# Experts of 65 to 128 tokens: the down projection as plain fp32 products, with only w1 and w3 split into high and low parts

## The chip, the cores and the metric

The kernel runs on one core of one Trainium2 chip. The metric is the device time in microseconds (us); the kernel before takes 2081.54 us, the median of three runs from 2077.73 to 2081.86 us. A change of about 0.2% of that, some 4 us, is what a measurement of this kernel can tell from no change.

## The reference, cut to what matters

Two layers of a token mixer and a channel mixer run over 256 context and 256 latent tokens of width 1024. The channel mixer of the second layer is a mixture of eight experts with the two best chosen for each token, and it is this part that the change touches:

```python
def swiglu(h, w1, w3, w2):
    return (jax.nn.silu(h @ w1) * (h @ w3)) @ w2

def moe_swiglu(h, w_r, w1e, w3e, w2e):
    logits = (h @ w_r).astype(jnp.float32)
    vals, idx = lax.top_k(logits, TOP_K)          # TOP_K = 2
    ...
    for e in range(N_EXPERTS):                    # 8
        out = out + comb[..., e:e + 1] * swiglu(h, w1e[e], w3e[e], w2e[e])
```

The inputs and weights are float32. Of one expert w1 and w3 are 1024 x 3584 and w2 is 3584 x 1024, so each expert brings 44 MB of weights.

## The kernel before, in words

The first part of the program, to about 1090 us, is everything up to the routing. After it come the eight experts, one after the other. For each expert the number of tokens that chose it (at most 256) is read into a register on every engine, and `by_width` branches to one of three programs: `few` for up to 64 tokens, `mid` for 65 to 128, and `big` for more. The code of all three is written out for each of the eight experts; an engine jumps over the ones it does not need. The code of one expert stands in the order few, mid, big.

The hidden width of 3584 is cut into seven blocks (`NB`) of 512 (`BLK`). A block has six pieces of weights of 128 x 2048 float32 words, 1 MiB each: pieces 0 to 3 are w1 and w3 for the two halves of the 1024 input rows, pieces 4 and 5 are the 512 rows of w2. SyncE (SP) loads them one by one into a ring of ten slots (`ESLOTS`), in the order of `ORDER` (lines 72 and 73), in which the two w2 pieces of block b-1 stand behind the four gate and up pieces of block b. A slot is loaded again when the matmuls that read it have ended (`wait_free`, line 532 and 536 are the two DMA issues). So the next expert's first ten pieces can land while the present one ends.

`mid` reaches float32 accuracy from TensorE's rounded format fp32r. A number is written as a high part, which is its value rounded to fp32r, and a low part, which is the rest; a product is then three products: high by high, low by high and high by low. For each of the 42 pieces of an expert

- ScalarE (ACT) copies the landed piece into one of three buffers `highs`, as rounded words (line 1370, `split`), once the piece used three before has been used up;
- VectorE (DVE) subtracts that from the piece in its place in the ring (line 1462, called by `split`), which leaves the low part there;
- TensorE (PE) runs `piece_product` (line 983 on): four times high by high (line 992) and low by high (line 994) from `highs`, and then four times high by low (line 999) from the ring. That is twelve matmuls of 128 x 128 weights by 128 x 512 moving words.

The order on PE within block b is: pieces 0 and 1 (`hidden(b, 0)`), four transposes of the gated hidden values of block b-1 (`turn`, line 1020), pieces 2 and 3 (`hidden(b, 1)`), and the two w2 pieces of block b-1 (`down`), which sum into the two banks `ps[0]` and `ps[1]` over all blocks. ACT applies the Silu (line 1376), DVE multiplies (line 1922) into `hid`; after the transposes ACT takes the high part `eh_high` from the bank (line 1380), and DVE the low part `eh_low` (line 1462 again, as a 128x512 form). At the end of an expert the order is: the first half of the next expert's gather (line 877), `turn` of the last block, `down` of the last two blocks, the second half of the gather, a transpose of the routing weights (line 884), and sixteen matmul records that spread the result over the tokens (line 902, `add_slots`), which need the copies of the two banks by ACT (line 1391) and DVE (line 1941).

`few` uses the pieces as they land, as fp32 products without any splitting: its gate and up matmuls are line 922, its down matmuls line 948. Its tiles have 64 columns of weights, and two of them stand beside each other in the array. In the runs' data three experts take `mid` (the first, the second and the fifth), five take `few`, none takes `big`.

Of the kernel before, what the change touches and what calls it, by code (L numbers as in the profile page):

```python
# [17 lines left out]
F32 = mybir.dt.float32  # L18
# [9 lines left out]
P = 128  # L28
D = 1024
# [36 lines left out]
BLK = 512  # L66
# [8 lines left out]
ORDER += [(NB - 1, 4), (NB - 1, 5)]  # L75
PLACE = {piece: n for n, piece in enumerate(ORDER)}
PER = len(ORDER)
HIGHS = 3

STEPS = 2 * NB  # L80
# [113 lines left out]
def hybrid_backbone(nc, x, c, ctx_in, c_ctx, w_mod, b_mod, g_mix_pre, g_mix_post, w_in, w_decay, b_decay, gla_norm,  # L194
# [23 lines left out]
    with ExitStack() as stack:  # L218
# [93 lines left out]
        spare_words = mixT[:, :, :].rearrange("p a b -> p (a b)")  # L312
        hid = spare_words[:, 0:2 * BLK].rearrange("p (a n) -> p a n", a=2)
        eh = spare_words[:, 2 * BLK:4 * BLK].rearrange("p (a n) -> p a n", a=2)
        rounded_words = x_high[:, :, :].rearrange("p a b -> p (a b)")
        eh_high = rounded_words[:, 2 * BLK:4 * BLK].rearrange("p (a n) -> p a n", a=2)
        eh_low = rounded_words[:, 4 * BLK:6 * BLK].rearrange("p (a n) -> p a n", a=2)
        highs = [x_low[:, 0:4, :].rearrange("p a b -> p (a b)"), x_low[:, 4:8, :].rearrange("p a b -> p (a b)"),
                 norms_r[:, 2:6, :].rearrange("p a b -> p (a b)")]

# [58 lines left out]
        high_ready = sem("high_ready")  # L379
        high_used = sem("high_used")  # L380
        low_ready = sem("low_ready")
        eh_low_ready = sem("eh_low_ready")
        sel_ready = sem("sel_ready")
        gather_ready = sem("gather_ready")
        xsel_vector = sem("xsel_vector")
# [174 lines left out]
        def _(pe):  # L560
# [345 lines left out]
            def few(e):  # L906

                H = FEW
                x = xsel
                pe.sem_inc(extra_ready, 3)  # L910
                pe.sem_inc(high_used, PER)

                def hidden(b, half):
                    acc = ps[2 + b % 2]
                    if half == 0 and b >= 2:
                        pe.wait_ge(hid_ready, e * STEPS + 2 * (b - 2) + 2)
                    for w in range(2):
                        wait_piece(pe, e, b, 2 * half + w)
                    for kk in range(4):
                        k = 4 * half + kk  # L920
                        for w in range(2):
                            ins = pe.matmul(acc[H * w:H * w + H, :], x[:, k, 0:H],  # L922
                                            piece_words(e, b, 2 * half + w)[:, kk * BLK:(kk + 1) * BLK],
                                            start=(k == 0), stop=(k == KD - 1), skip_group_check=True)
                            if kk == 3:
                                frees(ins, e, b, 2 * half + w)
                    if half == 1:
                        ins.then_inc(gu_ready, 2)

                def turn(b):  # L930

                    pe.wait_ge(hid_ready, e * STEPS + 2 * b + 2)
                    if b >= 2:
                        pe.wait_ge(eh_ready, e * STEPS + 2 * (b - 2) + 2)
                    for q in range(2):
                        ins = pe.transpose(ps[6 + b % 2][:, q * P:(q + 1) * P],  # L936
                                           hid[:, b % 2, q * P:(q + 1) * P], ident[:])
                    ins.then_inc(turn_ready, 2)

                def down(b):  # L940
                    pe.wait_ge(eh_ready, e * STEPS + 2 * b + 2)
                    for i in range(2):
                        wait_piece(pe, e, b, 4 + i)
                        for jj in range(2):
                            j = 2 * i + jj
                            for half in range(2):
                                o = jj * D + half * BLK
                                ins = pe.matmul(ps[0][H * half:H * half + H, :],  # L948
                                                eh[:, b % 2, ((j % 2) * 2 + j // 2) * H:][:, 0:H],
                                                piece_words(e, b, 4 + i)[:, o:o + BLK],  # L950
                                                start=(b == 0 and j == 0), stop=(b == NB - 1 and j == 3),
                                                skip_group_check=True)
                        frees(ins, e, b, 4 + i)
                    return ins

                pe.wait_ge(xsel_vector, e + 1)
                pe.wait_ge(xsel_scalar, e + 1)
                if e:
                    pe.wait_ge(sum_done, 4 * e)
                for b in range(NB):  # L960
                    hidden(b, 0)
                    if b:
                        turn(b - 1)
                    hidden(b, 1)
                    if b < NB - 1 and b:
                        down(b - 1)
                next_gather(e, 0)
                turn(NB - 1)
                down(NB - 2)
                down(NB - 1).then_inc(y_ready, STEPS)  # L970
                next_gather(e, 1)
                if e + 1 < NE:
                    turn_weights(e + 1)

                pe.wait_ge(y_vector, STEPS * (e + 1))
                pe.wait_ge(y_scalar, STEPS * (e + 1))
                add_slots(e, lambda s, m: yslot[H * (m // 4):H * (m // 4) + H, 0, (m % 4) * P:(m % 4 + 1) * P],
                          lambda s, m: swt_up[H:2 * H, :] if m // 4 else swt[0:H, e % 2, :], 1)

            def mid(e):  # L980
# [2 lines left out]

                def piece_product(b, i, outs, high, low, first, last):

                    n = e * PER + PLACE[b, i]
                    w_high_ = highs[n % HIGHS]
                    w_low_ = piece_words(e, b, i, ring_r)
                    pe.wait_ge(high_ready, n + 1)
# [25 lines left out]
                def turn(b):  # L1015
                    pe.wait_ge(hid_ready, e * STEPS + 2 * b + 2)
                    if b >= 2:
                        pe.wait_ge(eh_low_ready, e * STEPS + 2 * (b - 2) + 2)
                    for j in range(4):
                        ins = pe.transpose(ps[6 + b % 2][:, j * P:(j + 1) * P], hid[:, b % 2, j * P:(j + 1) * P],  # L1020
                                           ident[:])
# [1 line left out]

                def down(b):
                    pe.wait_ge(eh_ready, e * STEPS + 2 * b + 2)
                    pe.wait_ge(eh_low_ready, e * STEPS + 2 * b + 2)
                    for i in range(2):
                        js = [2 * i + q // 2 for q in range(4)]
                        ins = piece_product(b, 4 + i, [ps[q % 2][:] for q in range(4)],
                                            [eh_high[:, b % 2, j * P:(j + 1) * P] for j in js],  # L1030
                                            [eh_low[:, b % 2, j * P:(j + 1) * P] for j in js],
                                            2 if b == 0 and i == 0 else 0, 2 if b == NB - 1 and i == 1 else 0)
                    return ins

                pe.wait_ge(xsel_vector, e + 1)
# [21 lines left out]

            def big(e):

                pe.sem_inc(high_used, PER)  # L1060
                pe.wait_ge(xsel_vector, e + 1)
                pe.wait_ge(xsel_scalar, e + 1)
                if e:
# [84 lines left out]
        def _(act):  # L1148
# [193 lines left out]

            def few(e):
                H = FEW
                act.sem_inc(high_ready, PER)
                for b in range(NB):
                    act.wait_ge(gu_ready, e * STEPS + 2 * b + 2)
                    if b >= 2:
# [10 lines left out]
            def mid(e):  # L1359

                def split(n):

                    if n < PER:
                        b, i = ORDER[n]
                        at_ = e * PER + n
                        wait_piece(act, e, b, i)
                        if at_ >= HIGHS:
                            act.wait_ge(high_used, at_ - HIGHS + 1)
# [8 lines left out]

                def turned(b):
                    act.wait_ge(turn_ready, e * STEPS + 2 * b + 2)
                    act.copy(eh_high[:, b % 2, :], ps[6 + b % 2][:]).then_inc(eh_ready, 2)  # L1380

                for n in range(PER + 2):
                    split(n)
                    used = ORDER[n - 2] if n >= 2 else None
                    if used is not None and used[1] == 3:
                        gate(used[0])
                    if used is not None and used[1] == 1 and used[0]:
# [6 lines left out]

            def big(e):

                act.sem_inc(high_ready, PER)
                for b in range(NB):
                    for s in range(2):
                        act.wait_ge(gu_ready, e * STEPS + 2 * b + s + 1)  # L1400
# [22 lines left out]
        def _(dve):  # L1423
# [456 lines left out]
            def few(e):  # L1880
                H = FEW
                dve.sem_inc(extra_done, 3)
                dve.sem_inc(low_ready, PER)
                dve.sem_inc(eh_low_ready, STEPS)
                dve.wait_ge(swt_done, e + 1)
                dve.tensor_copy(swt_up[H:2 * H, :], swt[0:H, e % 2, :])
                for b in range(NB):
# [18 lines left out]
            def mid(e):  # L1906
                dve.sem_inc(extra_done, 3)

                def split(n):

                    if n < PER:
                        b, i = ORDER[n]
                        at_ = e * PER + n
                        dve.wait_ge(high_ready, at_ + 1)
                        low_part(piece_words(e, b, i, ring_r), piece_words(e, b, i),
                                 highs[at_ % HIGHS].bitcast(F32)).then_inc(low_ready, 1)
# [5 lines left out]
                    dve.tensor_tensor(hid[:, b % 2, :], esg[:, b % 2, :], ps[3 + 2 * (b % 2)][:],  # L1922
                                      ALU.mult).then_inc(hid_ready, 2)

                def turned(b):
                    dve.wait_ge(eh_ready, e * STEPS + 2 * b + 2)
                    low_part(eh_low[:, b % 2, :], ps[6 + b % 2][:],
                             eh_high[:, b % 2, :].bitcast(F32)).then_inc(eh_low_ready, 2)

                for n in range(PER + 2):  # L1930
                    split(n)
                    used = ORDER[n - 2] if n >= 2 else None
                    if used is not None and used[1] == 3:
                        gate(used[0])
                    if used == (2, 0) and e + 1 < NE:
                        select(e + 1)
                    if used is not None and used[1] == 1 and used[0]:
                        turned(used[0] - 1)
                turned(NB - 1)
                dve.wait_ge(y_ready, STEPS * (e + 1))  # L1940
                dve.tensor_copy(yslot[:, 0, 512:1024], ps[1][:]).then_inc(y_vector, STEPS)
                if e + 1 < NE:
# [3 lines left out]

            def big(e):

                dve.sem_inc(low_ready, PER)
                dve.sem_inc(eh_low_ready, STEPS)  # L1950
                for half in range(2):
                    dve.wait_ge(extra_ready, 3 * e + half + 1)
                    dve.tensor_copy(xsel2[:, 4 * half:4 * half + 4, :],
# [62 lines left out]
```

## Time and profile before

| what | value |
|---|---|
| median of three runs | 2081.54 us |
| the profiled execution: its own time | 2080.61 us |
| its span, first to last instruction | 2078.8 us |
| TensorE busy | 1827.6 us (88%) |
| VectorE busy | 844.4 us (41%) |
| ScalarE busy | 487.2 us (23%) |
| mean granted TensorE clock | 0.93 of 2.4 GHz |
| read from memory | 473.38 MB, 228 GB/s over the span |

A record of a matmul lasts from its start to its modelled end, which includes the way through the array, so successive matmuls overlap in the records; the distance between two starts is what a matmul costs in a row of them. An fp32 matmul has two records in the trace (and two weight loads), an fp32r matmul has one. "issue" as the releaser of an idle time says that the profile shows nothing that the engine waited for.

### The profile page before, as it was taken

What the parts mean: (1) busy time and instruction counts of PE and PEld (TensorE: products, weight loads), DVE (VectorE), ACT (ScalarE), POOL (GpSimd) and SP (SyncE); (2) the same over time, 40 slices, a digit from 0 to 9 for tenths busy, and PEclk for the clock granted to TensorE, in tenths of its full rate; (3) what the DMA queues carried; (4) which work ended last, traced back from release to release, by engine and by line L of the source; (5) the groups of instructions that cost most, each with busy time, mean ns of one, the idle gap of its engine ahead of it and who ended that gap; (6) DMA issues with size and microseconds to landing.
All of it is one profiled execution on the core that took longest, in us unless ns stands there. A gap on an engine that the chain in (4) does not pass through costs nothing.

```text
span 2078.8 us, 19529 instructions
## 1 busy us (share of the span) xinstructions
PE 1827.6 (88%) x7982; PEld 1131.9 (54%) x7982; DVE 844.4 (41%) x1212; ACT 487.2 (23%) x568; POOL 2.3 (0%) x12
## 2 busy tenths in 40 slices
PE   5998888969999999799779979997876998787886
PEld 2344444438888777348667868842324884232322
DVE  1243242073434466424448868820203882020102
ACT  3211023110000000221327747600002760000001
POOL 0000000000000000000000000000000000000000
PEclk9899999979999999899779999999998999999988
DMA  9323089142232220331237969979999997999994
GB/s 345 106 81 122 0 320 368 61 142 81 93 110 71 81 74 0 122 121 41 82 122 285 375 222 375 363 281 395 394 394 363 376 354 289 395 393 393 394 395 183
DMA packets 223827, 476.20 MB, mean 229 GB/s; under 512 B 9906, under 2 KB 32724, under 8 KB 223700
## 3 DMA queue, kind: packets, MB, share of 16 engines
q1 hardware_dynamic: 222176, 474.24, 62.3%
q8 instruction: 85, 1.39, 0.3%
q10 hardware_dynamic: 1524, 0.21, 0.1%
q14 instruction: 42, 0.34, 0.0%
HBM read 473.38 MB, written 1.05 MB: 228 GB/s over the span
## 4 chain that ended last, share of the span: by engine, by line
PE 70%; SPq 12%; DMA 7%; DVE 6%; issue 4%; ACT 2%; ACTq 0%; DVEq 0%; POOL 0%; POOLq 0%
PE ps L633 11%; SPq L532 9%; PE ps L639 6%; PE ps L640 6%; PE ps L641 6%; PE ps L992 6%; PE ps L994 6%; PE ps L922 5%; PE ps L999 5%; PE ps L794 4%; DMA ring<-in_e_w 4%; PE ps L685 3%; SPq L536 3%; DMA ring<-in_w_mod 3%; PE ps L588 3%
## 5 line engine op out<-in xcount | busy, mean ns | idle before, releaser
L922 PE MATMUL ps<-ring,work 128*64 128x512 f32 x1120 | 283.1, 655 | 83.1 <-DMA ring<-in_e_w 66.1
L633 PE MATMUL ps<-hT,ring 128*128 128x512 f32 (+2 forms) x672 | 246.9, 527 | 22.0 <-issue 12.3
L922 PEld LDWEIGHTS ps<-ring,work 128*64 128x64 f32 x1120 | 92.1, 149 | 250.0 <-issue 250.0
L633 PEld LDWEIGHTS ps<-hT,ring 128*128 128x128 f32 (+1 forms) x672 | 129.0, 196 | 137.5 <-issue 117.6
L1462 DVE TENSOR_TENSOR ring_rounded<-ring,hT_rounded 128x2048 fp32r<-128x2048 f32 x84 | 191.6, 2289 | 29.2 <-ACT hT_rounded L1370 22.0
L1894 DVE TENSOR_TENSOR mixT<-work,ps 64x256 f32<-64x256 f32 x70 | 29.7, 424 | 425.1 <-ACT work L1351 424.0
L1370 ACT CAST hT_rounded<-ring 128x2048 fp32r<-128x2048 f32 x84 | 159.9, 1911 | 45.0 <-PE ps L994 34.2
L639 PE MATMUL ps<-mixT_rounded,work_rounded 128*128 128x512 f32 x352 | 140.6, 399 | 10.6 <-DVE hT_rounded L1462 10.6
L641 PE MATMUL ps<-mixT_rounded,ring_rounded 128*128 128x512 f32 x352 | 139.1, 395 | 0.0
L640 PE MATMUL ps<-hT_rounded,work_rounded 128*128 128x512 f32 x352 | 139.1, 395 | 0.0
L948 PE MATMUL ps<-ring,mixT 128*64 128x512 f32 x560 | 125.8, 593 | 0.0
L992 PE MATMUL ps<-hT_rounded,work_rounded 128*128 128x512 f32 x252 | 102.2, 406 | 21.8 <-issue 18.6
L1462 DVE TENSOR_TENSOR ring_rounded<-ring,norms_rounded 128x2048 fp32r<-128x2048 f32 x42 | 96.1, 2289 | 22.7 <-ACT norms_rounded L1370 22.7
L994 PE MATMUL ps<-hT_rounded,work_rounded 128*128 128x512 f32 x252 | 100.2, 398 | 1.8 <-issue 1.8
L999 PE MATMUL ps<-ring_rounded,work_rounded 128*128 128x512 f32 x336 | 90.5, 391 | 0.2 <-DVE ring_rounded L1462 0.2
L794 PE MATMUL ps<-mixT,ring 128*128 128x512 f32 (+1 forms) x256 | 85.0, 486 | 1.2 <-issue 1.2
L1462 DVE TENSOR_TENSOR ring_rounded<-ring,work_rounded 128x1024 fp32r<-128x1024 f32 (+1 forms) x88 | 84.1, 956 | 1.5
L639 PEld LDWEIGHTS ps<-mixT_rounded,work_rounded 128*128 128x128 f32 x352 | 67.2, 191 | 30.0 <-DVE hT_rounded L1462 10.8
L948 PEld LDWEIGHTS ps<-ring,mixT 128*64 128x64 f32 x560 | 41.6, 137 | 76.1 <-issue 70.2
L1370 ACT CAST norms_rounded<-ring 128x2048 fp32r<-128x2048 f32 x42 | 80.3, 1913 | 9.3 <-issue 6.9
L588 PE MATMUL ps<-norms,ones 128*128 128x512 f32 (+1 forms) x144 | 69.0, 611 | 13.3 <-ACT norms L1178 13.2
L1353 ACT COPY mixT<-ps 128x256 f32<-128x256 f32 x35 | 13.0, 372 | 269.7 <-PE ps L936 269.7
(221 smaller groups left out, 2311.7 us busy)
## 6 DMA issues: line engine op xcount, KB each, us to landing
ring<-in_e_w SPq DMA_DIRECT2D x336, 1024.0 KB, 13.8
ring<-in_w_mod SPq DMA_DIRECT2D x24, 2048.0 KB, 15.9
ring<-in_w_in SPq DMA_DIRECT2D x12, 2048.0 KB, 11.8
ring<-in_w SPq DMA_DIRECT2D x22, 1024.0 KB, 7.8
ring<-in_w_out SPq DMA_DIRECT2D x4, 2048.0 KB, 13.9
ring<-in_w SPq DMA_DIRECT2D x4, 2048.0 KB, 7.8
ring<-in_w SPq DMA_DIRECT2D x2, 1536.0 KB, 6.5
mixT<-in_ctx SPq DMA_DIRECT2D x2, 512.0 KB, 4.2
```

Of the source, the lines that this page charges most:

```text
L532: sp.dma_start(dst.rearrange("p (k n) -> p k n", k=4), rows(w[0, e, k0 * P:(k0 + 4) * P], b * BLK, BLK)).then_inc(piece_in[s], 16)
L633: ins = pe.matmul(acc[0:width, 0:TOK - c0], w[:, k, m * P:m * P + width], hT[:, k, c0:], start=(k == 0), stop=(k == KD - 1))
L639: pe.matmul(acc, w_high_, x_high_, start=first, stop=False)
L640: pe.matmul(acc, w_high_, x_low_, start=False, stop=False)
L641: return pe.matmul(acc, w_low_, x_high_, start=False, stop=last)
L794: ins = pe.matmul(acc[:, 0:n], w[:, k, (m % 4) * P:(m % 4 + 1) * P], mixT[:, k, c0:], start=(i == 0), stop=(i == KD - 1))
L922: ins = pe.matmul(acc[H * w:H * w + H, :], x[:, k, 0:H], piece_words(e, b, 2 * half + w)[:, kk * BLK:(kk + 1) * BLK], start=(k == 0), stop ...
L992: pe.matmul(outs[q], high[q], w_high_[:, cols], start=q < first, stop=False, skip_group_check=True)
L994: ins = pe.matmul(outs[q], low[q], w_high_[:, cols], start=False, stop=False, skip_group_check=True)
L999: ins = pe.matmul(outs[q], high[q], w_low_[:, q * BLK:(q + 1) * BLK], start=False, stop=q >= 4 - last, skip_group_check=True)
L1370: act.copy(highs[at_ % HIGHS], piece_words(e, b, i)).then_inc(high_ready, 1)
L1462: return dve.tensor_tensor(dst, src, high, ALU.subtract)
```

## The change

Only the program `mid` changes in what it computes with. The gate and up pieces (w1 and w3) are split as before. The w2 pieces are no longer split: PE multiplies them as they lie in the ring, as fp32, by the transposed hidden values, which ACT now copies as plain float32 words into `eh`. The low part of the hidden values, its semaphore and DVE's step for it are gone. The counters of the splitting run over the 28 gate and up pieces (`SPLIT`) and not over all 42 (`PER`). The order of the pieces in the ring, their loading, and the order of the steps on PE stay.

```diff
+SPLIT = len(GATE_UP)
...
 (TensorE, mid)
                 def turn(b):
                     pe.wait_ge(hid_ready, e * STEPS + 2 * b + 2)
                     if b >= 2:
-                        pe.wait_ge(eh_low_ready, e * STEPS + 2 * (b - 2) + 2)
+                        pe.wait_ge(eh_ready, e * STEPS + 2 * (b - 2) + 2)
...
                 def down(b):
                     pe.wait_ge(eh_ready, e * STEPS + 2 * b + 2)
-                    pe.wait_ge(eh_low_ready, e * STEPS + 2 * b + 2)
                     for i in range(2):
-                        js = [2 * i + q // 2 for q in range(4)]
-                        ins = piece_product(b, 4 + i, [ps[q % 2][:] for q in range(4)],
-                                            [eh_high[:, b % 2, j * P:(j + 1) * P] for j in js],
-                                            [eh_low[:, b % 2, j * P:(j + 1) * P] for j in js],
-                                            2 if b == 0 and i == 0 else 0, 2 if b == NB - 1 and i == 1 else 0)
+                        wait_piece(pe, e, b, 4 + i)
+                        for jj in range(2):
+                            j = 2 * i + jj
+                            for half in range(2):
+                                o = jj * D + half * BLK
+                                ins = pe.matmul(ps[half][:], eh[:, b % 2, j * P:(j + 1) * P],
+                                                piece_words(e, b, 4 + i)[:, o:o + BLK],
+                                                start=(b == 0 and j == 0), stop=(b == NB - 1 and j == 3),
+                                                skip_group_check=True)
+                        frees(ins, e, b, 4 + i)
                     return ins
...
 (ScalarE, mid)
                 def split(n):
-                    if n < PER:
-                        b, i = ORDER[n]
-                        at_ = e * PER + n
+                    if n < SPLIT:
+                        b, i = GATE_UP[n]
+                        at_ = e * SPLIT + n
...
                 def turned(b):
                     act.wait_ge(turn_ready, e * STEPS + 2 * b + 2)
-                    act.copy(eh_high[:, b % 2, :], ps[6 + b % 2][:]).then_inc(eh_ready, 2)
-
-                for n in range(PER + 2):
+                    act.copy(eh[:, b % 2, :], ps[6 + b % 2][:]).then_inc(eh_ready, 2)
+
+                for n in range(SPLIT + 2):
                     split(n)
-                    used = ORDER[n - 2] if n >= 2 else None
+                    used = GATE_UP[n - 2] if n >= 2 else None
...
 (VectorE, mid)
-                def turned(b):
-                    dve.wait_ge(eh_ready, e * STEPS + 2 * b + 2)
-                    low_part(eh_low[:, b % 2, :], ps[6 + b % 2][:],
-                             eh_high[:, b % 2, :].bitcast(F32)).then_inc(eh_low_ready, 2)
-
-                for n in range(PER + 2):
+                for n in range(SPLIT + 2):
```

## Rows read from the trace of the kernel before

**Rows 1.** The page: span, engines' busy time, DMA issues of the experts' weights.
```profile
span 2078.8 us, 19529 instructions
PE 1827.6 (88%) x7982; PEld 1131.9 (54%) x7982; DVE 844.4 (41%) x1212; ACT 487.2 (23%) x568; POOL 2.3 (0%) x12
...
ring<-in_e_w SPq DMA_DIRECT2D x336, 1024.0 KB, 13.8
```

**Rows 2.** Busy time by engine in stretches; the last three columns are clock, DMA share, GB/s.
```profile
core 0: us, PE busy (x) PEld busy (x) DVE busy (x) ACT busy (x) POOL busy (x), PEclk, DMA share, GB/s
1160.00:1200.00 40.00, 40.00 (x183) 33.07 (x182) 35.88 (x20) 28.31 (x18) 0.00 (x0) 1.00 1.02 376
...
1400.00:1440.00 40.00, 30.30 (x132) 11.03 (x132) 1.70 (x4) 2.29 (x5) 0.00 (x0) 0.96 1.04 395
...
1098.80:1221.10 122.30, 120.28 (x548) 99.17 (x549) 104.07 (x60) 84.87 (x56) 0.00 (x0) 1.00 0.95 346
...
1369.80:1587.30 217.50, 180.36 (x800) 70.48 (x800) 26.71 (x57) 17.74 (x35) 0.00 (x0) 0.93 1.01 381
```

**Rows 3.** Waits of TensorE over the first `mid` expert: total, times, longest.
```profile
PE ps L992 <- issue: 1.4, 1, 1.4
PE ps L1020 <- DVE mixT L1922: 0.4, 1, 0.4
PE ps L999 <- DVE ring_rounded L1462: 0.2, 1, 0.2
```

**Rows 4.** Timeline, TensorE in a steady `mid` block: start, duration, line.
```profile
1132.93 0.48 PE L992 MATMUL ps<-hT_rounded,work_rounded 128*128 128x512 f32 x1
...
1137.59 1.07 PE L999 MATMUL ps<-ring_rounded,work_rounded 128*128 128x512 f32 x4
...
1140.31 1.07 PE L999 MATMUL ps<-ring_rounded,mixT_rounded 128*128 128x512 f32 x4
...
1149.73 0.48 PE L992 MATMUL ps<-hT_rounded,work_rounded 128*128 128x512 f32 x1
```

**Rows 5.** Timeline, fp32 matmuls of layer 0's output projection, full clock.
```profile
373.24 7.03 PE L794 MATMUL ps<-mixT,ring 128*128 128x512 f32 x16
380.11 1.02 PE L588 MATMUL ps<-norms,ones 128*128 128x512 f32 x2
```

**Rows 6.** Timeline, down matmuls of a `few` expert.
```profile
1409.08 3.63 PE L948 MATMUL ps<-ring,mixT 128*64 128x512 f32 x16
```

**Rows 7.** Timeline, TensorE at the end of the first `mid` expert.
```profile
1205.71 1.95 PE L877 MATMUL ps<-work 128*128 128x128 f32 x16
1208.06 0.65 PE L1020 MATMUL ps<-ident,mixT 128*128 128x128 f32 x4 [0.41 <-DVE mixT L1922]
...
1213.12 1.07 PE L999 MATMUL ps<-ring_rounded,mixT_rounded 128*128 128x512 f32 x4
1215.58 0.47 PE L992 MATMUL ps<-hT_rounded,mixT_rounded 128*128 128x512 f32 x1 [1.39 <-issue]
```

**Rows 8.** The same end, on ScalarE and VectorE.
```profile
1212.46 0.57 ACT L1380 CAST mixT_rounded<-ps 128x512 fp32r<-128x512 f32 x1
1212.59 2.29 DVE L1462 TENSOR_TENSOR ring_rounded<-ring,norms_rounded 128x2048 fp32r<-128x2048 f32 x1 [1.92 <-ACT norms_rounded L1370]
1214.80 0.68 DVE L1462 TENSOR_TENSOR mixT_rounded<-ps,mixT_rounded 128x512 fp32r<-128x512 f32 x1
```

**Rows 9.** TensorE's first matmuls of the experts 1, 2, 4 and 5, with the idle time ahead.
```profile
1234.66 0.76 PE L992 MATMUL ps<-hT_rounded,work_rounded 128*128 128x512 f32 x1 [7.56 <-issue]
1369.78 12.22 PE L922 MATMUL ps<-ring,work 128*64 128x512 f32 x48 [3.62 <-issue]
1598.26 0.77 PE L992 MATMUL ps<-hT_rounded,work_rounded 128*128 128x512 f32 x1 [11.00 <-issue]
1731.70 12.22 PE L922 MATMUL ps<-ring,work 128*64 128x512 f32 x48 [3.79 <-issue]
```

**Rows 10.** Waits of the DMA queue SP over the expert part.
```profile
SPq L532 <- PE ps L999: 280.8, 84, 43.6
SPq L536 <- PE ps L999: 104.6, 42, 4.0
```

**Rows 11.** ScalarE's split of a piece and ScalarE's Silu in the steady state.
```profile
1133.75 1.92 ACT L1370 CAST norms_rounded<-ring 128x2048 fp32r<-128x2048 f32 x1
1138.74 0.60 ACT L1376 ACTIVATE work<-ps 128x512 f32<-128x512 f32 x1 [1.26 <-issue]
```

More of the change, by code:

```diff
@@ L314, in hybrid_backbone @@
         eh = spare_words[:, 2 * BLK:4 * BLK].rearrange("p (a n) -> p a n", a=2)
-        rounded_words = x_high[:, :, :].rearrange("p a b -> p (a b)")
-        eh_high = rounded_words[:, 2 * BLK:4 * BLK].rearrange("p (a n) -> p a n", a=2)
-        eh_low = rounded_words[:, 4 * BLK:6 * BLK].rearrange("p (a n) -> p a n", a=2)
         highs = [x_low[:, 0:4, :].rearrange("p a b -> p (a b)"), x_low[:, 4:8, :].rearrange("p a b -> p (a b)"),
@@ L381, in hybrid_backbone @@
         low_ready = sem("low_ready")
-        eh_low_ready = sem("eh_low_ready")
         sel_ready = sem("sel_ready")
@@ L910, in few @@
                 pe.sem_inc(extra_ready, 3)
-                pe.sem_inc(high_used, PER)
+                pe.sem_inc(high_used, SPLIT)
                 def hidden(b, half):
@@ L984, in piece_product @@
                 def piece_product(b, i, outs, high, low, first, last):
-                    n = e * PER + PLACE[b, i]
+                    n = e * SPLIT + GATE_UP.index((b, i))
                     w_high_ = highs[n % HIGHS]
@@ L1058, in big @@
             def big(e):
-                pe.sem_inc(high_used, PER)
+                pe.sem_inc(high_used, SPLIT)
                 pe.wait_ge(xsel_vector, e + 1)
@@ L1344, in few @@
                 H = FEW
-                act.sem_inc(high_ready, PER)
+                act.sem_inc(high_ready, SPLIT)
                 for b in range(NB):
@@ L1395, in big @@
             def big(e):
-                act.sem_inc(high_ready, PER)
+                act.sem_inc(high_ready, SPLIT)
                 for b in range(NB):
@@ L1882, in few @@
                 dve.sem_inc(extra_done, 3)
-                dve.sem_inc(low_ready, PER)
-                dve.sem_inc(eh_low_ready, STEPS)
+                dve.sem_inc(low_ready, SPLIT)
                 dve.wait_ge(swt_done, e + 1)
@@ L1909, in split @@
                 def split(n):
-                    if n < PER:
-                        b, i = ORDER[n]
-                        at_ = e * PER + n
+                    if n < SPLIT:
+                        b, i = GATE_UP[n]
+                        at_ = e * SPLIT + n
                         dve.wait_ge(high_ready, at_ + 1)
@@ L1923, in gate @@
                                       ALU.mult).then_inc(hid_ready, 2)
-                def turned(b):
-                    dve.wait_ge(eh_ready, e * STEPS + 2 * b + 2)
-                    low_part(eh_low[:, b % 2, :], ps[6 + b % 2][:],
-                             eh_high[:, b % 2, :].bitcast(F32)).then_inc(eh_low_ready, 2)
-                for n in range(PER + 2):
+                for n in range(SPLIT + 2):
                     split(n)
-                    used = ORDER[n - 2] if n >= 2 else None
+                    used = GATE_UP[n - 2] if n >= 2 else None
                     if used is not None and used[1] == 3:
@@ L1936, in mid @@
                         select(e + 1)
-                    if used is not None and used[1] == 1 and used[0]:
-                        turned(used[0] - 1)
-                turned(NB - 1)
                 dve.wait_ge(y_ready, STEPS * (e + 1))
@@ L1947, in big @@
             def big(e):
-                dve.sem_inc(low_ready, PER)
-                dve.sem_inc(eh_low_ready, STEPS)
+                dve.sem_inc(low_ready, SPLIT)
                 for half in range(2):
```

## The prediction, made before the changed kernel had run

> **What bounds the kernel now.** I read the page first, to see which engine is busiest: TensorE (PE) at 88%, and eight experts that load 336 MiB-sized pieces, 42 each [rows 1]. That average mixes two kinds of expert, so next come the stretches [rows 2]. In a `few` expert the DMA moves 395 GB/s at a share of 1.04 and PE is busy 30 of 40 us: the load of weights sets the pace. In a `mid` expert PE is busy 40.0 of 40.0 us at a clock of 1.00 (the 2.4 GHz level), while the DMA moves 376 GB/s and 346 over the whole first expert. So here PE sets the pace, but not by much: a block of six pieces is 6.29 MB, which at 395 GB/s is 15.9 us, and PE takes 1149.73 - 1132.93 = 16.80 us for it [rows 4]. PE's waits settle it: over the first `mid` expert nowhere does PE wait for a DMA, and its waits on VectorE (DVE) and for nothing visible sum to 2.0 us [rows 3]; the other way round SP waits 385 us for matmuls of line 999 to free slots [rows 10]. DVE is at 35.9 of 40 us and ScalarE (ACT) at 28.3 [rows 2]; both wait for PE's use of the buffers, so their work counts only where PE waits for them.
>
> **What the change takes from PE.** Per block `down` runs two pieces of twelve fp32r matmuls. A piece takes 1140.31 - 1137.59 = 2.72 us [rows 4], 0.227 us a matmul. Two pieces are 5.44 us.
>
> **What it adds to PE.** Per block 8 fp32 matmuls of 128x128 by 128x512, 16 records. The same shape stands in layer 0 at full clock: 16 records fill 380.11 - 373.24 = 6.87 us [rows 5], 0.859 us a matmul. These have their own weight load in each record too, so it is inside the figure. Operands of the same kind (one tile of weights for two halves, other banks) give no reason for another rate, and I take 6.87 us. Net per block: 6.87 - 5.44 = +1.43 us. There are seven blocks in each of three `mid` experts: 21 x 1.43 = +30.0 us.
>
> The bounds: below, two fp32 matmuls with 64 columns of weights run beside each other in `few`, 16 records in 3.63 us [rows 6]; that needs half-width tiles, which `down` of `mid` has not. Above, a full-width fp32 matmul could cost four times an fp32r one as these run here, 4 x 0.227 = 0.907 us, so 7.25 us a block, +1.81, and 21 x 1.81 = +38.1. The row of the same shape is the nearest, so 0.859 stands. The trace shows 0.859 / 0.227 = 3.79 fp32r matmuls for one fp32 matmul, against the three that the split form uses. The Trainium skill (FP8 and Floating Point Precision, TensorE Precision Notes) says that true fp32 makes four passes through the array where the reduced form makes one, which speaks against this change; the trace nearly agrees, and by the rule at fp32r's distance the net would be that upper 38.1.
>
> **What it takes from ACT and DVE.** Two copies of 1.92 us from ACT [rows 11], two subtractions of 2.29 us and one of 0.68 from DVE [rows 8] per block, 5.3 us of DVE. In the steady block PE waits for neither, so 18 of these 21 blocks gain nothing. At an expert's end they do matter. DVE is in the subtraction of a w2 piece when the last gate is due; `turn` of the last block waits 0.41 us for it [rows 7]. Then, between `down` of block 5 and `down` of block 6, PE stands still: the last line 999 group starts at 1213.12 and would pass on after 4 x 0.227 = 0.91 us, at 1214.03, but the next matmul starts at 1215.58 [rows 7], 1.55 us late. What it waits for is the low part of the hidden values, which DVE takes only at 1214.80, behind the split of the first w2 piece, ending at 1215.48 [rows 8]. Both waits go: ACT's float copy follows the transposes at once and is done some 6 us before `down` of block 6, which stands behind 6.87 us of matmuls. The three `mid` experts look alike here, so 3 x (1.55 + 0.41) = -5.9 us. What is late next is nothing on ACT or DVE: with three buffers of high parts and 28 pieces, they get three pieces ahead during each `down`; a gate-up piece then asks 2.29 of DVE per 2.72 us of PE and of ACT 1.92, and the gates' 0.68 and 0.60 us [rows 8, 11] fit in the 6.87 us of `down`.
>
> **The DMA and the slots.** Issue order and count stay. A w2 piece is now freed after its own 3.43 us of matmuls in place of 2.72, so PE asks for a block each 18.23 us where the DMA needs 15.9: nothing new waits there, and SP's waits on PE grow. Nor does a `few` expert give it back: it begins with a full ring before and after, and runs at 395 GB/s already. So the sum stays on the path.
>
> **Sum.** +30.0 - 5.9 = +24.1 us. On the profiled execution: span 2078.8 to 2102.9, its own time 2080.6 to 2104.7. The median of the runs is 0.9 above that execution, so 2105.6 us.
>
> **Rivals.**
> (a) The gate-up matmuls get faster, since DVE and ACT touch memory less. An fp32r matmul takes 0.227 us and one record pass of fp32 half of 0.429, so 0.215: if all 48 fp32r matmuls left in a block fell to that, 48 x 0.012 x 21 = -12.1 us, +12 in all, 2093.5. For it: the split form alone has the longer distance. Against: nothing says that the other engines cause it, since PE's starts are as regular where DVE pauses.
> (b) The four stalls behind a branch. PE stands 7.56, 3.62, 11.0 and 3.79 us before its first matmul of the next expert, mostly for nothing that the profile shows [rows 9]; the code of `mid` gets shorter, and where it lies moves. The spread between like branches (3.6 to 11.0) is 7.4 us; two such moves the wrong way give +24 + 15 = +39, 2120, the right way +9, 2091. The Trainium skill (Runtime: NRT & Kernel Launch, Instruction fetch mechanics) says that a taken branch out of the fetched window makes the engine wait for its code; the stalls fit that, and no row tells how the shorter code would change them.
> (c) The other side, faster: fp32 matmuls on neighbouring banks overlap as in [rows 6], 3.63 us for a block's `down`. PE would need 16.80 - 5.44 + 3.63 = 15.0 us a block, the DMA's 15.9 decides, and 21 x (16.80 - 15.9) = 19 us go: 2063. It decides if 16 records take under 5.4 us. Against it: [rows 5] shows full-width ones, one behind the other.
> (d) No change: the DMA is the real bound and covers a slower PE. It would need DMA waits on PE in `mid`; [rows 3] has none. 2081.5.
>
> **How the numbers follow.** Forecast 0.82 (2098 to 2114, the upper end by the 0.907 us bound with the end's gain: +32), (a) 0.06, (b) 0.07, of which half is above the range, (c) 0.03, (d) 0.02. Range 2094 to 2115. Slower by over 0.2% holds the forecast, (a) and (b): 0.95; same 0.02; faster 0.03. The 0.2%, 4 us, is what a measurement of this kernel can tell.
>
> **What would show it.** Right: line 992, 994 and 999 with 336 records each in place of 504, 336 new records of an fp32 matmul from the ring at a distance of 0.43 us, a steady block of 18.2 us, the DMA rate in a `mid` stretch down to about 6.29 MB / 18.2 us = 345 GB/s, the stop before the last `down` gone, DVE near 25 of 40 us, the `few` stretches as long as before. Wrong: a block of 16 us or less (c), a distance below 0.22 us between gate-up matmuls (a), other stalls ahead of the first matmul of an expert (b), PE waiting for DMA or for DVE in the steady block.

## The result, and the profile after

The changed kernel takes 2100.81 us, the median of five runs (2099.38 to 2105.08), against 2081.54 for the kernel before beside it: a ratio of 1.0095, 95% interval 1.0077 to 1.0112, so 16 to 23 us slower. Five more runs on another occasion gave 1.012 (1.0102 to 1.0137), 21 to 29 us. The +24.1 us that was forecast lies 1 us above the first interval and inside the second. The profiled execution's span went from 2078.8 to 2103.2 us, +24.4; that execution, at 2105.08 us, was the slowest of its five.

The page of the changed kernel, its first lines and the group of the new down matmuls (line, engine, operation, tiles, count, busy time, mean ns):

```profile
span 2103.2 us, 19020 instructions
PE 1865.7 (89%) x7814; PEld 1099.7 (52%) x7814; DVE 738.0 (35%) x1149; ACT 409.2 (19%) x526; POOL 2.3 (0%) x12
...
L1030 PE MATMUL ps<-ring,mixT 128*128 128x512 f32 x336 | 147.1, 592 | 0.0
```

VectorE lost 106 us of work and ScalarE 78, against [rows 1], and PE gained 38 us of recorded busy time: work left two engines that had waited and came to the one that had not.

A steady block of the changed kernel on PE (timeline; the records of a few matmuls in between are left out):

```profile
1135.67 0.60 PE L1018 MATMUL ps<-ident,mixT 128*128 128x128 f32 x4
...
1141.60 7.03 PE L1030 MATMUL ps<-ring,mixT 128*128 128x512 f32 x16
...
1150.29 1.07 PE L997 MATMUL ps<-ring_rounded,work_rounded 128*128 128x512 f32 x4
...
1153.01 1.07 PE L997 MATMUL ps<-ring_rounded,work_rounded 128*128 128x512 f32 x4
1153.92 0.60 PE L1018 MATMUL ps<-ident,mixT 128*128 128x128 f32 x4
```

From `turn` to `turn` a block is 1153.92 - 1135.67 = 18.25 us, against 16.80 in [rows 4]. Sixteen fp32 records last 7.03 us from the first start to the last modelled end, to the hundredth what line 794 showed in [rows 5]. A gate-up piece still takes 2.72 us.

The stretch of the changed kernel that answers to [rows 2], same columns:

```profile
1160.00:1200.00 40.00, 40.00 (x145) 26.41 (x145) 22.50 (x13) 19.38 (x14) 0.00 (x0) 1.00 0.98 351
```

PE is full and at the 2.4 GHz level, as before. DVE fell from 35.9 to 22.5 of 40 us, the DMA from 376 to 351 GB/s, since PE asks for less.

The end of the first expert, and the first matmul of the next, which answer to [rows 7] and [rows 9]:

```profile
1214.57 1.95 PE L875 MATMUL ps<-work 128*128 128x128 f32 x16
...
1216.35 0.60 PE L1018 MATMUL ps<-ident,mixT 128*128 128x128 f32 x4
1216.79 13.90 PE L1030 MATMUL ps<-ring,mixT 128*128 128x512 f32 x32
1230.52 1.95 PE L875 MATMUL ps<-work 128*128 128x128 f32 x16
...
1244.40 0.76 PE L990 MATMUL ps<-hT_rounded,work_rounded 128*128 128x512 f32 x1 [7.91 <-issue]
```

Both `down` run as one group of 32 records; neither the wait ahead of `turn` nor the stop ahead of the last `down` is left.

Where the 24.4 us of the two profiled spans lie, each `mid` expert from its first matmul to the second half of the gather:

| stretch | before | after | more |
|---|---|---|---|
| expert 0 (mid) | 1098.85 to 1221.14 | 1100.54 to 1230.52 | 7.7 |
| expert 1 (mid) | 1234.66 to 1360.19 | 1244.40 to 1376.07 | 6.1 |
| expert 4 (mid) | 1598.26 to 1721.95 | 1614.23 to 1745.32 | 7.4 |
| all the rest | | | 3.2 |

The three `mid` experts hold 21.2 us. The rest is 1.7 ahead of the experts, 0.4 between experts 0 and 1, 0.1 from expert 1's gather to expert 4 and 1.0 behind expert 4, outside the products that were changed. The same three stretches in the second profile of the changed kernel are 130.01, 131.84 and 130.94 us, 21.3 in sum over the kernel before, while its stretch ahead of the experts is 1.0 us shorter than before: that part varies from execution to execution.

### The profile page after: what moved, and what is told of

It is laid out like the page before. It is cut to its first block, busy times and chain, and to the rows that moved or that the text cites. A ratio compares the mean times of both kernels' runs of the same rounds, so it can differ in the third digit from the quotient of the medians.

```text
span 2103.2 us, 19020 instructions
## 1 busy us (share of the span) xinstructions
PE 1865.7 (89%) x7814; PEld 1099.7 (52%) x7814; DVE 738.0 (35%) x1149; ACT 409.2 (19%) x526; POOL 2.3 (0%) x12
## 4 chain that ended last, share of the span: by engine, by line
PE 72%; SPq 11%; DMA 6%; DVE 6%; issue 3%; ACT 1%; ACTq 0%; DVEq 0%; POOL 0%; POOLq 0%
PE ps L631 11%; SPq L530 8%; PE ps L1030 7%; PE ps L920 6%; PE ps L637 6%; PE ps L639 6%; PE ps L638 6%; DMA ring<-in_e_w 4%; PE ps L792 4%; PE ps L990 4%; PE ps L992 4%; PE ps L997 4%; PE ps L683 3%; SPq L534 3%; PE ps L586 3%
## 5 line engine op out<-in xcount | busy, mean ns | idle before, releaser
L920 PE MATMUL ps<-ring,work 128*64 128x512 f32 x1120 | 292.2, 672 | 74.9 <-DMA ring<-in_e_w 58.1
L631 PE MATMUL ps<-hT,ring 128*128 128x512 f32 (+2 forms) x672 | 246.5, 526 | 22.5 <-issue 12.3
L1464 DVE TENSOR_TENSOR ring_rounded<-ring,hT_rounded 128x2048 fp32r<-128x2048 f32 x57 | 129.8, 2290 | 108.3 <-ACT hT_rounded L1372 107.4
L1030 PE MATMUL ps<-ring,mixT 128*128 128x512 f32 x336 | 147.1, 592 | 0.0
L638 PE MATMUL ps<-hT_rounded,work_rounded 128*128 128x512 f32 x352 | 139.1, 395 | 0.0
L1372 ACT CAST hT_rounded<-ring 128x2048 fp32r<-128x2048 f32 x57 | 107.9, 1906 | 95.9 <-issue 70.4
L990 PE MATMUL ps<-hT_rounded,work_rounded 128*128 128x512 f32 x228 | 96.7, 424 | 21.3 <-issue 18.1
L1030 PEld LDWEIGHTS ps<-ring,mixT 128*128 128x128 f32 x336 | 63.5, 190 | 73.0 <-issue 71.8
L992 PE MATMUL ps<-hT_rounded,work_rounded 128*128 128x512 f32 x228 | 90.7, 398 | 0.0
L637 PEld LDWEIGHTS ps<-mixT_rounded,work_rounded 128*128 128x128 f32 x352 | 67.2, 191 | 29.8 <-DVE hT_rounded L1464 10.8
L639 PEld LDWEIGHTS ps<-mixT_rounded,ring_rounded 128*128 128x128 f32 x352 | 67.3, 191 | 14.3
```

The source lines that it names most:

```text
L631: ins = pe.matmul(acc[0:width, 0:TOK - c0], w[:, k, m * P:m * P + width], hT[:, k, c0:], start=(k == 0), stop=(k == KD - 1))
L637: pe.matmul(acc, w_high_, x_high_, start=first, stop=False)
L638: pe.matmul(acc, w_high_, x_low_, start=False, stop=False)
L639: return pe.matmul(acc, w_low_, x_high_, start=False, stop=last)
L920: ins = pe.matmul(acc[H * w:H * w + H, :], x[:, k, 0:H], piece_words(e, b, 2 * half + w)[:, kk * BLK:(kk + 1) * BLK], start=(k == 0), stop ...
L990: pe.matmul(outs[q], high[q], w_high_[:, cols], start=q < first, stop=False, skip_group_check=True)
```

## Experiments

The theory: PE alone sets the pace in a `mid` expert; the fp32 form costs it 1.43 us a block, and the work taken from ScalarE and VectorE counts only at two stops at an expert's end. The rivals: the splitting slows PE in other ways; the price is per expert and not per block; the DMA decides.

**Only the end of an expert, with everything still split.** In the loops of ScalarE and VectorE over the pieces:

```diff
                 for n in range(PER + 2):
+                    if n == PER - 3:          # VectorE alone
+                        gate(NB - 1)
+                    if n == PER - 1:          # both
+                        turned(NB - 1)
                     split(n)
...
-                    if used is not None and used[1] == 3:
+                    if used is not None and used[1] == 3 and used[0] < NB - 1:      # VectorE alone
...
-                turned(NB - 1)
```

> The kernel before, split down projection and all; only the order on ScalarE and VectorE at the end of a mid expert changes: VectorE gates the last block before it splits the second w2 piece of block 5, and both take the last transposed hidden values before they split the last w2 piece. Theory (PE stands still 1.55 us ahead of the last down and about 0.5 us ahead of the last turn, only because of this order): both stops go in three experts, 3 x (1.55 + 0.5) = 6 us less than the kernel before, ratio 0.997, steady block unchanged at 16.80 us. Rival (the stops are TensorE's own, or the splits come too late in turn): no change, the wait moves to the split of the last piece.

Measured: 0.9973 of the kernel before (0.9963 to 0.9984), 2074.71 us; by the ratio 5.6 us less. Its timeline on PE, the gathers' halves at the end of the first expert:

```profile
1203.11 1.95 PE L877 MATMUL ps<-work 128*128 128x128 f32 x16
...
1216.26 1.95 PE L877 MATMUL ps<-work 128*128 128x128 f32 x16
```

13.15 us between them, 15.43 in the kernel before (1205.71 [rows 7] to 1221.14): 2.28 us an expert, 6.8 in three, where 6 were expected. So the stops at the end were a matter of the order on the two helpers, and could be had without any fp32 product.

**fp32 products in the last block alone, or in all but the last.** The program of before with `SPLITS`, the pieces that are split, in place of `ORDER`, and with both forms of `down`:

```diff
+PLAIN = (6,)                       # or (0, 1, 2, 3, 4, 5)
+SPLITS = [p for p in ORDER if p[1] < 4 or p[0] not in PLAIN]
...
                 def down(b):
...
+                    if b in PLAIN:
+                        ...        # the fp32 form of the changed kernel
+                        return ins
```

> The kernel before with fp32 products of w2 in the last block (block 6) alone; blocks 0 to 5 are split. Theory: 3 x 1.43 = 4.3 us more on PE, 3 x 1.55 = 4.7 us less by the stop ahead of the last down, the 0.5 us wait of the last turn stays: within 1 us of the kernel before. Rival (the fp32 form itself is the dearer part everywhere and gains nothing at the end): 4.3 us more.

Measured: 0.9995 (0.9985 to 1.0005), 1 us less, within 3 less and 1 more: no change that can be told, as expected, and not the rival's +4.3.

> The kernel before with fp32 products of w2 in blocks 0 to 5, the last block split. The splits of its two w2 pieces no longer stand behind the use of block 5's, so they are done early. Theory: 18 x 1.43 = 25.7 us more on PE, 4.7 us less by the stop ahead of the last down: +21 us on the kernel before, ratio 1.010, and the changed kernel +24 by the same count less the last turn's wait. Rival (a fixed cost or gain per expert, in the branches, rather than a price per block): the same +20 as with all seven blocks, or nothing like 18/21 of it.

Measured: 1.0088 (1.0073 to 1.0103), +18 us (15 to 21), at the lower side of the +21. The stretch between the halves of the gather is 15.17 us in the one and 15.18 in the other: in both, one of the two last `down` is fp32 and the stop is gone. 15.43 + 1.43 - 1.55 would be 15.31. The interval of the second run overlaps the changed kernel's, so the run times alone do not tell 18 blocks from 21. The traces do: from first matmul to second half of the gather the three `mid` experts take 122.00, 122.87 and 123.10 us with one fp32 block each, and 129.20, 130.87 and 130.66 with six. The 15 blocks more cost 22.8 us, 1.52 each. The time goes by the number of fp32 blocks, and not by the expert.

**All the helpers' work given back.** PE does the products of the changed kernel; ScalarE and VectorE split the w2 pieces and the hidden values too, and PE waits for that. The edit is shown for one of these steps:

```diff
-                        low_part(piece_words(e, b, i, ring_r), piece_words(e, b, i),
+                        low_part(piece_words(e, b, i, ring_r) if i < 4 else highs[at_ % HIGHS], piece_words(e, b, i),
                                  highs[at_ % HIGHS].bitcast(F32)).then_inc(low_ready, 1)
```

> TensorE as in the changed kernel, fp32 products of the landed w2. ScalarE and VectorE do all of the splitting of the kernel before again: w2 pieces too (the low part goes into the buffer of the high part and is not used), and the low part of the hidden values, unused; PE waits for each. Theory (the work taken from ScalarE and VectorE is worth nothing but at the ends): the steady block stays at 18.24 us, only the last turn's 0.5 us wait comes back, so +0 to +3 us on the changed kernel, +20 to +26 on the one before; gate-up matmuls at 0.227 us in both. Rival (the splits slow PE, by contention or by waits): the block grows beyond 18.5 us and the time by 6 us or more over the changed kernel's.

Measured: 1.0114 (1.0097 to 1.0131), +24 us, between the two measurements of the changed kernel. The steady block, the end of the first expert (last the low part of its last hidden values on VectorE), and the stretch that answers to [rows 2]:

```profile
1135.23 0.60 PE L1020 MATMUL ps<-ident,mixT 128*128 128x128 f32 x4
...
1153.48 0.60 PE L1020 MATMUL ps<-ident,mixT 128*128 128x128 f32 x4
...
1216.47 0.66 PE L1020 MATMUL ps<-ident,mixT 128*128 128x128 f32 x4 [0.39 <-DVE mixT L1932]
1216.96 13.99 PE L1036 MATMUL ps<-ring,mixT 128*128 128x512 f32 x32
...
1223.07 0.68 DVE L1472 TENSOR_TENSOR mixT_rounded<-ps,mixT 128x512 fp32r<-128x512 f32 x1
```

```profile
1160.00:1200.00 40.00, 40.00 (x145) 26.41 (x145) 32.87 (x19) 27.93 (x19) 0.00 (x0) 1.00 0.99 351
```

DVE works 32.9 us in 40 here and 22.5 in the changed kernel, ACT 27.9 and 19.4, and the block is 18.25 us in both. The 5.3 us of VectorE and 3.8 of ScalarE in each block are worth nothing in the steady state. The wait of the last `turn` is back. With it the three experts take 2.4 us more than in the changed kernel's profile (130.69, 132.00 and 132.41 us). The stop ahead of the last `down` is not back, though PE waits for the low part again: VectorE has it at 1223.75, and the 6.87 us of products of block 5 that began at 1216.96 last until 1223.83. So that stop would have gone with the low part kept, covered by the longer fp32 products.

**Half of the fp32 matmuls, and twice as many.** `for jj in range(1)` in `down` of `mid` leaves half of the second product's sum out; a loop `for again in range(2)` around the matmul doubles it.

> The changed kernel with every fp32 matmul of down in mid experts run twice (the sum is doubled). Theory (fp32 products cost 0.859 us each, and nothing hides them): 21 x 6.87 = +144 us on the changed kernel, about 2245 us, the steady block 25.1 us. Rival (part of the price is a fixed cost of passing between the two number formats, or hidden): less than +135 us.

Measured: 1.0817 (1.0798 to 1.0837), +170 us on the kernel before, which is 145 to 150 over the changed kernel by its two ratios (its span is 147.4 over the changed one's). Its steady block:

```profile
1139.66 0.60 PE L1018 MATMUL ps<-ident,mixT 128*128 128x128 f32 x4
1145.57 13.89 PE L1031 MATMUL ps<-ring,mixT 128*128 128x512 f32 x32
1164.76 0.60 PE L1018 MATMUL ps<-ident,mixT 128*128 128x128 f32 x4
```

25.10 us, 6.85 over the changed kernel's 18.25: 0.856 us for each fp32 matmul, the second eight as dear as the first, so no fixed part shows. 21 such blocks are 143.9 us, as expected; the other 3.5 of the 147.4 us lie outside this sum.

> The changed kernel with half of the fp32 matmuls of down in mid experts left out (every second group of 128 hidden rows; the pieces are loaded all the same). PE's own time for a block falls by 3.43 us, to 14.8 us, below the DMA's 15.9. Theory A (every us of PE in mid counts, also below 15.9, since the ten slots fill while PE passes from expert to expert): 21 x 3.43 = 72 us less than the changed kernel, less a few us that the following few experts wait for a ring that is not full: 65 to 72 less, about 2032 us. Theory B (as priced in the prediction's rival c: the DMA's 15.9 us decides in each block): 21 x 2.3 = 48 us less, about 2053 us.

Measured: 0.9793 (0.9776 to 0.981), 43 us under the kernel before, so 63 to 68 under the changed one (62.1 by the spans): at or under the lower end of the 65 to 72 of theory A. Theory B, 48, falls. The timeline of the first expert's end, the next experts' first matmuls, and a stretch of expert 1:

```profile
1206.33 1.95 PE L875 MATMUL ps<-work 128*128 128x128 f32 x16
...
1223.11 0.77 PE L990 MATMUL ps<-hT_rounded,work_rounded 128*128 128x512 f32 x1 [10.81 <-issue]
...
1343.42 12.65 PE L920 MATMUL ps<-ring,work 128*64 128x512 f32 x48 [6.40 <-issue]
...
1572.47 0.76 PE L990 MATMUL ps<-hT_rounded,work_rounded 128*128 128x512 f32 x1 [10.82 <-issue]
...
1692.28 12.30 PE L920 MATMUL ps<-ring,work 128*64 128x512 f32 x48 [6.47 <-issue]
```

```profile
1260.00:1300.00 40.00, 40.00 (x160) 29.11 (x159) 26.86 (x15) 22.98 (x16) 0.00 (x0) 1.00 1.04 395
```

From its first matmul at 1100.35 the first expert takes 105.98 us, 24.0 less than in the changed kernel and just 7 x 3.43: PE never waits for a piece, though the DMA is at its 395 GB/s. It works off the ten slots within the expert and refills them while PE passes to the next. What is missing to 72 us stands ahead of the first matmuls: 10.81, 6.40, 10.82 and 6.47 us, where the changed kernel has 7.91, 3.68, 10.14 and 3.60, 9.2 us in sum. 72 - 9.2 = 62.8. So what was missing was not a wait of the `few` experts for the ring, as expected. Inside the stalls of 7.91 and 3.68 us the changed kernel's trace has no packet of the ring's queue; inside those of 10.81 and 6.40 us that queue has 61% and 99.9% of the DMA engines' time. The stalls are longer where the ring is still being filled while PE passes on.

**The branches.** The kernel before, with the branch turned round, so that the code of `mid` stands first:

```diff
-    with eng.If(chosen < FEW + 1):
-        few()
-    with eng.Else():
+    with eng.If(chosen > FEW):
         with eng.If(chosen < P + 1):
             mid()
         with eng.Else():
             big()
+    with eng.Else():
+        few()
```

> The kernel before with only the order of the branches changed: the code of mid (and big) stands ahead of that of few for each expert. Theory (the stall of 7.6 to 11 us ahead of a mid expert's first matmul is the engine's wait for code behind a branch, and depends on how the branch goes): the stalls ahead of the mid experts 1 and 4 get shorter by some 3 to 7 us each, those ahead of the few experts 2 and 5 longer; the steady blocks stay at 16.80 us. In all within -12 to +8 us of the kernel before. Rival (the stall is a wait for data, the buffers or the sums of the expert before): stalls and time unchanged, 2081 us.

Measured: 0.9976 (0.9964 to 0.9988), 2077.94 against 2082.88 us, 5 us less. The first matmuls of experts 1, 2, 4 and 5:

```profile
1227.27 0.77 PE L992 MATMUL ps<-hT_rounded,work_rounded 128*128 128x512 f32 x1 [3.93 <-issue]
...
1365.89 12.54 PE L922 MATMUL ps<-ring,work 128*64 128x512 f32 x48 [7.96 <-issue]
...
1585.57 0.77 PE L992 MATMUL ps<-hT_rounded,work_rounded 128*128 128x512 f32 x1 [0.98 <-DVE work L1877]
...
1722.72 12.87 PE L922 MATMUL ps<-ring,work 128*64 128x512 f32 x45 [8.03 <-issue]
```

Against [rows 9] the stall went from 7.56 to 3.93, 3.62 to 7.96, 11.00 to 0.98 and 3.79 to 8.03 us, 5.1 less in sum. Expert 4's went down by 10.0 us, more than the 3 to 7 expected. The data, the buffers and the sums are the same, so the rival falls: it is the way to the code that PE waits for.

The DMA table of the profile shows packets of the kind "instruction", of 16 and 8 KB each, apart from the ring's queue (q1). Queue, kind, packets, MB and share of the 16 engines, for four stretches: the stall of 7.56 us before (1227.10 to 1234.66), 10 us in the middle of a `mid` expert before (1140 to 1150), and with `mid` first the stalls of 0.98 us (1584.59 to 1585.57) and 7.96 us (1357.93 to 1365.89):

```profile
q8 instruction: 2, 0.03, 2.1%
q14 instruction: 1, 0.01, 0.4%
...
q1 hardware_dynamic: 1827, 3.89, 104.1%
...
q1 hardware_dynamic: 192, 0.38, 105.8%
...
q8 instruction: 2, 0.03, 2.1%
q14 instruction: 4, 0.03, 1.4%
q1 hardware_dynamic: 8, 0.03, 0.9%
```

In these two traces each of the seven stalls of 3.6 us or more has one to three packets of q8 in it, and the stall of 0.98 us has none. By the Trainium skill (Runtime: NRT & Kernel Launch, Instruction fetch mechanics), a taken branch whose target lies outside the window fetched ahead has to wait until DMA has fetched the target's code; the packets in the stalls, and the longer stalls beside a full ring queue, agree with that. Which engine each packet is for, and how the stall divides between fetch and branch, no row shows.

**The two gains together, and the changed kernel again.**

> The kernel before with the two edits that gained by themselves: the earlier steps of ScalarE and VectorE at the end of a mid expert (0.9973 alone) and the code of mid ahead of that of few (0.9976 alone). Theory (they take away different stops of PE, one inside an expert's end and one behind its branch): the gains add, ratio 0.995, about 11 us less, 2070 to 2073 us. Rival (the earlier end only moves the wait into the branch, which waits for the same thing): the ratio stays at 0.997.

Measured: 0.9953 (0.9939 to 0.9968), 2071.78 against 2081.93 us: the gains add (0.9973 x 0.9976 = 0.9949). Its trace has both, 13.16 us between the gather's halves and stalls of 3.54, 7.97, 0.98 and 7.89 us. This version beats both kernels, by 10 and by some 32 us.

> The changed kernel once more, beside the kernel before on one chip, to have its price from more runs. Theory (+30.0 us of fp32 products, -6 us at the ends, from which a stall behind a branch may take or give up to 3): +21 to +24 us in the profiled span, ratio 1.009 to 1.012.

Measured: 1.012 (1.0102 to 1.0137), 2104.45 against 2081.93 us, its span 2101.7 us, 22.9 over the kernel before: inside what was expected.

## Why the prediction was right

- **PE bounds `mid`.** Right. Matmuls added or taken from PE moved the time by their own length (double, half), and a third less work on the helpers moved the steady block by nothing.
- **-5.44 and +6.87 us a block.** Right: 18.25 - 16.80 = 1.45 measured against 1.43. The row of another stage with the same shape gave the price.
- **-5.9 us at the ends.** Right in place, a little small, and in part for another reason: both stops are gone, but the one ahead of the last `down` would have been covered by the longer fp32 products with the low part kept too. The wait ahead of `turn` was 0.57 us, not 0.41: from the gather to `turn` 2.35 us went to 1.78. The idle time that the profile gives begins at a modelled end and is less than the distance of the starts tells. In all the end section grew from 15.43 to 15.95 us where 2.86 - 1.96 = 0.90 more were expected, 0.4 an expert less. VectorE was at 22.5 of 40 us where near 25 was forecast, the DMA at 351 GB/s where 345 was.
- **What was not in the sum.** In expert 1 the kernel before stops for 1.76 us after its first matmul (line 994, for nothing visible); the changed kernel does not, nor does any experiment but the first (1.65). Why is open. So 30.4 - 5.9 - 1.1 - 1.8 = 21.6, beside 21.2 measured in the three experts, and 3.2 elsewhere make up the 24.4. That the span met the forecast to 0.3 us is in part chance: 3.2 us came from elsewhere, and the median, 2100.81 us, is 4.8 under the 2105.6 forecast. The price of the change is the 21 us of the experts.
- **Rival (a)**, faster gate-up matmuls, is out: 2.72 us a piece with DVE at 22.5 us in 40, and the same with DVE at 32.9. What makes 0.227 us of them, where half an fp32 record pair would be 0.215, stays open.
- **Rival (b)**, the stalls behind branches, is real, but moved by under 1 us each (7.91, 3.68, 10.14, 3.60 in the changed kernel), apart from the 1.8 us above. The prediction's spread of 7.4 us "between like branches" compared unlike ones: the two into `mid` stood 7.56 and 11.0 us, the two into `few` 3.62 and 3.79. And the stalls do show something, the packets of kind "instruction".
- **Rival (c)**, overlap of fp32 matmuls, is out, by the 7.03 us group. Its price was wrong too: it let the DMA's 15.9 us decide in each block, but half of the matmuls went below that and PE waited for no piece. With ten slots and some 13 us of passing between experts the DMA's floor holds over an expert and not over a block; at 14.8 us a block the gain was whole, apart from the 9 us that the branches took.
- **Rival (d)** is out: no wait for a DMA on PE in `mid`.

## What to carry to other kernels

Count passes on the engine that is full, at the distance of starts and not by the length of records: an fp32 matmul cost 3.8 of the rounded ones here, so three rounded products were cheaper, as long as the splitting fits beside them on engines that wait anyway. A stop on the critical engine at the end of a loop is often an order of steps on a helper; put the step that releases it ahead of the one that nobody needs yet before changing the arithmetic. And price a floor over the stretch that the buffers span.

## What the runs showed of the hardware

PE stood 3.6 to 11 us behind a branch into or out of `mid`. Which code stood first moved that to 0.98 us for one (a `few` expert followed by a `mid` one) and to 8.0 for others, with the same data. Beside a ring queue that was still busy the same branch cost 10.8 us in place of 7.9, and 6.4 in place of 3.7. The order of branches is worth 5 us of 2081 here, and it depends on which expert follows which.

A stall also leaves a slow start. In the changed kernel the granted clock is 0.50, the 1.2 GHz level, from 1244.40 to 1247 behind the stall of 7.91 us, and the matmuls stand 0.43 us apart instead of 0.227; from 1250 on it is 1.00. The first expert of the same kernel starts at 1.00 (1100.54 to 1103). This goes with the 1.7 us by which expert 1 takes longer than expert 0 in the changed kernel (131.67 and 129.98).
